# Starting the operands of the large matmuls at multiples of 256 bytes of SBUF

## The reference

```python
# first block
hn = rmsnorm(x);            proj = hn @ w_in            # 2048 x 1856, then state space and attention
h = x + [ssm | attention] @ w_out                       # 2048 x 2048
a = rmsnorm(h) @ w_up                                   # 2048 x 11264, causal convolution of 3
h = h + (silu(gate) * val) @ w_down                     # 5632 x 2048;  x = rmsnorm(h)
# second block
P = rmsnorm(x) @ w_in                                   # 2048 x 11744, then SSD and RWKV-7 mixers
h = x + [y_ssd | y_rwkv] @ w_out                        # 4096 x 2048
h = h + (silu(v @ w_gate) * (v @ w_up)) @ w_down        # v = rmsnorm(h), 2048 x 5632 twice, 5632 x 2048
return rmsnorm(h)
```

## Time and profile before

| | before |
|---|---|
| median of 3 runs | 2955.93 us (2955.74 to 2959.97) |
| profiled execution, first to last instruction | 2954.4 us |
| TensorE matmuls busy | 2857.8 us, 97% |
| VectorE busy | 2039.6 us, 69% |
| ScalarE busy | 1552.7 us, 53% |
| GpSimd busy | 724.2 us, 25% |
| DMA queue of the weights | 45.0% of 16 engines' time |

### The profile page before, as it was taken

How to read it: one execution, slowest core, us unless ns; L and a number is a source line. 1 busy time by engine, 2 the same in 40 slices (tenths; PEclk the granted TensorE clock), 3 DMA queues, 4 the chain that set the end, 5 groups by cost and what they waited for, 6 DMA issues and landing times.

```text
span 2954.4 us, 52371 instructions
## 1 busy us (share of the span) xinstructions
PE 2857.8 (97%) x21074; PEld 2538.4 (86%) x21074; DVE 2039.6 (69%) x3273; ACT 1552.7 (53%) x2574; POOL 724.2 (25%) x870
## 2 busy tenths in 40 slices
PE   8989999999999998999899999999999999999998
PEld 8868988888888888888788888997888888888887
DVE  6675887765777667777777776777766665566654
ACT  7345555544555554566556655465445444444443
POOL 0342211200112230776456630003121110011112
PEclk9999999999999999999999999999999999999999
DMA  6314555556555555422222223454555555655554
GB/s 248 104 59 156 174 197 186 191 174 205 189 195 186 175 196 179 143 91 94 80 94 94 105 94 120 154 185 157 185 183 189 192 188 174 207 194 186 185 181 148
DMA packets 80046, 475.38 MB, mean 161 GB/s; under 512 B 8256, under 2 KB 11328, under 8 KB 38720
## 3 DMA queue, kind: packets, MB, share of 16 engines
q1 hardware_dynamic: 76768, 459.72, 45.0%
q10 hardware_dynamic: 3040, 12.32, 1.2%
HBM read 465.72 MB, written 6.29 MB: 160 GB/s over the span
## 4 chain that ended last, share of the span: by engine, by line
PE 78%; DVE 10%; ACT 4%; POOL 4%; issue 3%; DMA 0%; SPq 0%; POOLq 0%; ACTq 0%; DVEq 0%
PE bank L769 36%; PE bank L773 22%; PE bank L771 5%; PE bank L772 4%; PE bank L762 3%; DVE m L1307 2%; ACT m L2200 2%; POOL m L2933 2%; POOL m L2929 1%; DVE m L1353 1%; DVE m L1975 1%; PE bank L1103 1%; PE bank L1215 0%; PE bank L1107 0%; PE bank L866 0%
## 5 line engine op out<-in xcount | busy, mean ns | idle before, releaser
L773 PE MATMUL bank<-m,m 128*128 128x256 f32 x6624 | 1860.5, 281 | 0.0
L769 PE MATMUL bank<-m,m 128*128 128x512 f32 x4736 | 1650.0, 393 | 10.8 <-DVE m L2072 5.7
L1307 DVE TENSOR_TENSOR m<-m,m 128x1024 fp32r<-128x1024 f32 (+1 forms) x912 | 1033.1, 1141 | 569.9 <-ACT m L2200 563.5
L773 PEld LDWEIGHTS bank<-m,m 128*128 128x128 f32 x6624 | 1252.2, 189 | 0.2
L2200 ACT ACTIVATE m<-m 128x1024 fp32r<-128x1024 f32 (+1 forms) x912 | 877.7, 976 | 641.8 <-PE bank L773 615.4
L769 PEld LDWEIGHTS bank<-m,m 128*128 128x128 f32 x4736 | 890.7, 188 | 211.0 <-DVE m L2072 5.9
L771 PE MATMUL bank<-m,m 128*128 128x256 f32 x1888 | 561.2, 297 | 23.5 <-DVE m L1307 20.1
L772 PE MATMUL bank<-m,m 128*128 128x256 f32 x1888 | 534.6, 283 | 0.0
L771 PEld LDWEIGHTS bank<-m,m 128*128 128x128 f32 x1888 | 361.6, 192 | 43.4 <-issue 31.3
L772 PEld LDWEIGHTS bank<-m,m 128*128 128x128 f32 x1888 | 361.8, 192 | 1.3
L2909 POOL TENSOR_TENSOR m<-m,m 128x256 fp32r<-128x256 f32 x44 | 63.4, 1441 | 547.7 <-ACT m L2491 547.7
(11 more groups left out here) (375 smaller groups left out, 2830.5 us busy)
## 6 DMA issues: line engine op xcount, KB each, us to landing
m<-in_w_up SPq DMA_DIRECT2D x88, 1024.0 KB, 4.8
m<-in_w_down SPq DMA_DIRECT2D x128, 704.0 KB, 4.0
m<-in_w_gu SPq DMA_DIRECT2D x88, 1024.0 KB, 4.8
m<-in_w_out SPq DMA_DIRECT2D x48, 1024.0 KB, 5.1
m<-in_w_krv SPq DMA_DIRECT2D x48, 1024.0 KB, 4.8
m<-in_w_xbc SPq DMA_DIRECT2D x24, 1024.0 KB, 4.8
m<-in_w_z SPq DMA_DIRECT2D x16, 1024.0 KB, 4.8
m<-in_w_in SPq DMA_DIRECT2D x14, 1024.0 KB, 6.1
```

The costliest lines, as they stand in the source:

```text
L769: pe.matmul(bank.rearrange("p (a b) -> p a b", a=2), hi, x, start=kc == L.k0, stop=False)
L773: m = pe.matmul(ps, lo, x[:, 0, :], start=False, stop=last)
L1307: v.tensor_tensor(lo_of(k), raw_of(k)[0], hi_of(k).bitcast(F32), SUB).then_inc(*lo_v(("lo", k)))
```

## The change: what it does

```diff
-NTOT = 57040
+NTOT = 56992
 NARENA = NTOT - RAW * SLOT - 2 * CUT * PIECE
...
         w12, omm = alloc(16), alloc(52)
+        top[0] += -(BASE // 4 + top[0]) % 64
         base = top[0]
         hno = top[0]
         hnr = alloc(2, 16, T, dt=F32R)
...
         top[0] = bufo + 3 * 2560
+        top[0] += -(BASE // 4 + top[0]) % 64
         sdo = top[0]
         xd = alloc(2, 2048)
```

## The result

| | before | changed |
|---|---|---|
| median of 4 runs | 2956.35 us (2955.74 to 2959.97) | 2985.12 us (2981.55 to 2986.92) |
| profiled execution, first to last instruction | 2954.4 us | 2979.7 us |

The ratio is 1.0094, with a 95% interval from 1.0082 to 1.0106: the change makes the kernel slower by 28.8 us. The forecast was 2834 us, its range ended at 2962. The sign is that of the rival with a chance of 0.16, which gave 2997 us.

The account below looks back on a forecast made before the run. TensorE's block pace was taken as the bound in the feed-forwards. Gains of 97.5 (wide), 8.2 and 16.0 us (narrow) sum to 121.7, taken from 2955.9 for 2834 us; eight-in-ten range 2800 to 2962 us.

Parts of the forecast that it names:

- What bounds the kernel: TensorE is saturated in both feed-forwards, so their 1466 us is the number of blocks times the pace of one.
- The size of the excess: Over columns and fixed costs, 20.2 ns for each wide block and 7.1 ns for each narrow matmul.
- The excess is what a 17th piece would cost: Activation runs of 1024 bytes starting 32 behind a multiple of 64 touch 17 pieces; alignment saves 6.7 ns a run.
- The 97.5 us for wide blocks: Gain from aligned activations in wide blocks: 90.5 us over 4480 blocks plus 7.0 us over the 256 reading `ysr`.
- the narrow 24.2: Gain in narrow blocks: 8.2 us in full for 384, 16.0 us for the other 1504 at start and in mixers, counted half.
- The chance of 0.54: Chance given to the forecast itself, 2834 us, with its likeliest case's own range 2805 to 2865 us.
- `ysr`'s 353.3 ns: Wide blocks of the `w_out2` half reading `ysr` take 353.3 ns against 346, cited as showing that an address counts.
- the rival of half the gain: Excess has two sources, activations' start and interplay with weight loads, and one stays: 61 us gained, 2895 us; chance 0.14.
- It doesn't go with the weight loads: Excess follows columns, not the two loads of wide or three of narrow blocks; moving weights gains nothing.
- The slower rival: Weights and activations at equal remainders collide, wide blocks go to 353.3 ns: +41 us, 2997 us; chance 0.16.
- The rule of 16-byte lines: SBUF reads: by the skill's 16-byte lines both kernels read equally many full lines, so no gain, 2956 us.
- Hidden work: Loads, ScalarE's copies and VectorE's halves stay hidden at no cost; pieces later than 2.61 us would set the pace.

Follow-up runs that it names:

- sweep_wide: TensorE alone runs wide blocks at 24 address settings, computing none of the reference; 346.6 to 353.6 ns a block, no whole-kernel time.
- weights_only: Kernel before with only weights and halves moved from 192 to 0 modulo 256, activations unmoved; 2975.49 us, ratio 1.0062.
- activations_only: Changed kernel with weights and halves moved back to 192, so only activations differ from before; 2976.35 us, ratio 1.0069.
- sweep_narrow: Narrow blocks alone at eight distances, with smaller loads, and whole float32 matmuls, computing none of the reference; 340.0 to 360.0 ns a narrow block with full loads.
- aligned_weights_96: Changed kernel with weights' buffers 160 bytes lower, at 96 modulo 256, activations still aligned; 2951.85 us, ratio 0.9984 to the kernel before.
- wide grid: `grid_wide`: wide blocks alone at 512 combinations of three distances, each entered once, computing none of the reference; three at 340.0 ns, none lower.
- sweep_columns: Single matmuls of 64 to 512 columns, each with its own load, plus repeated column or weight; 512 columns took 234.2 ns at distance 160.

## Why the prediction was wrong, point by point

- **What bounds the kernel: right.** The pace of the blocks carried the change into the span: +25.7 us of TensorE's busy time, +25.3 us of span, with VectorE's and ScalarE's halves as long as before.
- **The size of the excess: right for wide blocks, too large for narrow ones.** 346.7 ns stand against 325.8 by columns and fixed costs; with one column read over and over, 512 and 256 columns take 215.8 and 111.7 ns, together 327.5. But three matmuls of 256 would take 335.0 ns that way, and no narrow block anywhere took less than 340.0, and the text took the narrow blocks down by 21.3 ns each, from 350 to below 329.
- **The step that failed: "The excess is what a 17th piece would cost".** The text took 6.7 ns a run for 16 columns, these for 64 bytes, and activations 32 behind a multiple of 64 for the cause. `sweep_wide` ran activations at multiples of 64 and 256 with weights at 0, 64 and 192: 346.6 ns at best, where the forecast needed 326. The 97.5 us for wide blocks were nothing, and the narrow 24.2 with them. In their place the runs show a pace that goes with the distance from the weights' start to the activations', and that cost 28.8 us here. The chance of 0.54 rested on one agreement of sizes, and the text said itself that it had no row of the other case.
- **A clue that was read and not followed.** `ysr`'s 353.3 ns was used as evidence that an address counts. It has the same remainder modulo 64 as `hnr`, 32, so it spoke against the piece of 64 bytes as the whole cause, which the text granted only in the rival of half the gain. Taken as 160 - 192 against 96 - 192, distances of 224 and 160, it is the first two rows of the table of distances.
- **"It doesn't go with the weight loads": right for the common part, wrong for the rest.** The weights moved alone change 346.7 to 350.0 ns (`weights_only`). The forecast took nothing for the weights' move; it costs 20 us by itself.
- **The slower rival: right in sign, and in its size partly by luck.** It asked whether the two streams disturb each other at equal remainders. They do interact, but equality isn't the cause: `weights_only` and `activations_only` have no equal pair and lose 20 us each. The wide price of 6.7 ns a block (it took 7.3) and the narrow one of 5.6 (it took 7) were about right. But distance 0 isn't the worst for wide blocks: 64, 192 and 224 are at 353 nearly always, while 0 has two paces, of which 346.7 is as good as before. The changed kernel ran the first 1760 wide blocks at the fast one, and 1760 x 6.7 ns is 11.7 us, about what lies between the rival's +41 and the measured +28.8.
- **The rule of 16-byte lines.** The Trainium skill, page "SBUF — State Buffer", section "Specifications (TRN2)", made both kernels equal. That no start of the activations takes the excess away agrees with it; that 346.7 goes to 353.3 ns at equal line use doesn't. The Trainium skill, page "TensorE: Matmul & The Clock Gate", section "Step-by-step: what each phase is for", says that loading the next weights doesn't steal read bandwidth from the running matmul, whose port is its own. The pace's dependence on the distance to the weights (346.6 to 353.4 ns in `sweep_wide`), and on the bytes of a load (352 to 340 ns in `sweep_narrow`), doesn't fit that sentence; the 18 ns that a matmul of 512 columns keeps with a load from one address agree with it.
- **Hidden work: not put to the test.** VectorE's halves, the loads and ScalarE's copies did not become late, but the pace at which the text asked about them, 2.61 us a piece, never came.

**What is shown and what stays open.** Shown: the pace depends on the distance modulo 256 and on the kind of block, with no other engine at work, and a kernel's time follows when only the weights' start is changed (2985.12 to 2951.85 us by one number, `aligned_weights_96`). Shown too: the distance doesn't fix the pace alone. Wide blocks have two paces at 0, 64 and 224, narrow ones at 128, 160 and 192, by the stretch or its entry. The common excess was found only where the activations' addresses change at a column a cycle at the upper clock. Open: why a distance counts at all, what picks one of two paces, and what the common excess is; that loads and reads meet in some shared unit is an argument, no more. The sweeps and grids are one execution each.

## What to carry to other kernels

Where TensorE is saturated, compute the pace from columns and clock, and compare it with the distance between starts: a difference of 2% is invisible in a busy share of 97%. Before buffers are aligned, list both operands' addresses modulo 256 and look at their difference, not at either one; the best difference is that of one shape, so measure it with a small kernel for each shape that matters, entered in several ways, and again in the whole kernel: of the best combination of the wide grid, 340.0 ns, the whole kernel held one quarter of one feed-forward. And when a size fits a mechanism neatly, look for the row in the trace that has the same cause and another effect; here it had been quoted.

## What the runs showed of the hardware that was not expected

- Float32r matmuls with a load of their own have a floor in `sweep_columns`: 111.7 ns at the upper clock for 64 and 192 columns and for one column read 256 times, 213.3 ns at the lower for 64, 128 and 192. 256 columns at changing addresses take 113.3 to 120.
- The granted clock fell to 0.5 three times in `sweep_columns`, at 135.7, 241.5 and 343.9 us, each time while matmuls of 64 columns or the short ones before them ran, and rose again during stretches of 192 columns.
- One pair of addresses, two paces: 346.7 or 353.3 ns at distance 0, in one kernel and one execution, kept for hundreds of blocks (1760 and 2112 in the changed kernel); narrow blocks at distance 192, 340.0 or 353.3.
- Whole float32 blocks show no such step between the two distances tried: 431.6 ns a pair at 160 and 0.
